# Four up pieces of a feed-forward layer with their products split into halves of the array's rows

## The reference, cut to what matters

```python
h = _causal_depthwise_conv(x @ w_up[l], conv_w[l], conv_b[l])     # w_up: 1024 x 5632, conv over 3 tokens
a, u = jnp.split(h, 2, axis=-1)
ffn = (jax.nn.gelu(a, approximate=False) * u) @ w_down[l]
x = _layer_norm(DEEPNORM_ALPHA * x + ffn, ln_ffn_g[l], ln_ffn_b[l])
```

## Time and profile before

| | |
|---|---|
| median of 3 runs | 1567.59 us (1564.45 to 1567.66) |
| the profiled execution | 1566.09 us, of which the span of the trace is 1564.3 us |
| PE busy | 1515.6 us, 97% of the span |
| DVE, ACT, POOL busy | 1022.0, 691.9 and 435.9 us |
| pieces 4 to 9 of the up projection | 423.63 to 488.91 us from the span's start, six times 10.88 us |

### The profile page before, as it was taken

The page is one execution under the profiler, slowest core; times in us unless marked ns, Lnnn a source line. Parts: engine busy times, 40 slices in busy tenths (PEclk is TensorE's granted clock), DMA queues, the critical chain, the costliest instruction groups (busy, mean ns, idle before and its releaser), DMA issues. The chain is left out here.

```text
span 1564.3 us, 21018 instructions
## 1 busy us (share of the span) xinstructions
PE 1515.6 (97%) x8432; PEld 1300.6 (83%) x8432; DVE 1022.0 (65%) x1547; ACT 691.9 (44%) x1020; POOL 435.9 (28%) x367
## 2 busy tenths in 40 slices
PE   5999998999999999999999999998999999999997
PEld 5778886788888888888988888886788999999886
DVE  7676457769677866678643643338855799985334
ACT  5644346755533354233523344443445544543322
POOL 0024315621511211000260032214342666660002
PEclk9999999999999999999999999999999999999999
DMA  8342112363244523665424332314462123224211
GB/s 310 109 148 92 64 55 95 133 221 118 108 163 161 178 91 121 244 252 204 133 108 148 108 98 91 118 49 161 142 234 87 53 109 109 107 108 162 85 78 54
DMA packets 50987, 203.61 MB, mean 130 GB/s; under 512 B 18528, under 2 KB 18784, under 8 KB 32138
## 3 DMA queue, kind: packets, MB, share of 16 engines
q1 hardware_dynamic: 37346, 172.04, 30.7%
q0 software_dynamic: 8576, 28.29, 5.1%
q10 hardware_dynamic: 4968, 1.94, 0.5%
HBM read 181.24 MB, written 21.00 MB: 129 GB/s over the span
## 5 line engine op out<-in xcount | busy, mean ns | idle before, releaser
L583 PE MATMUL ps<-xl,whi 128*128 128x512 f32 (+1 forms) x1136 | 393.1, 346 | 0.0
L1853 DVE TENSOR_TENSOR wlo<-raw,whi 128x2048 fp32r<-128x2048 f32 x89 | 221.8, 2493 | 142.7 <-ACT whi L1212 142.5
L1212 ACT ACTIVATE whi<-raw 128x512 fp32r<-128x512 f32 (+1 forms) x191 | 232.4, 1223 | 127.6 <-PE ps L584 84.3
L582 PE MATMUL ps<-xh,whi 128*128 128x256 f32 (+1 forms) x768 | 262.4, 342 | 6.2 <-DVE xl L1897 6.2
L584 PE MATMUL ps<-xh,wlo 128*128 128x256 f32 (+1 forms) x768 | 256.8, 334 | 0.0
L583 PEld LDWEIGHTS ps<-xl,whi 128*128 128x128 f32 x1136 | 216.2, 190 | 24.2
L582 PEld LDWEIGHTS ps<-xh,whi 128*128 128x128 f32 x768 | 146.8, 191 | 28.3 <-issue 15.6
L584 PEld LDWEIGHTS ps<-xh,wlo 128*128 128x128 f32 x768 | 146.7, 191 | 14.8
L582 PE MATMUL ps<-xhr,whi 128*128 128x512 f32 (+1 forms) x368 | 136.8, 372 | 0.7 <-DVE xl L1897 0.7
L584 PE MATMUL ps<-xhr,wlo 128*128 128x512 f32 (+1 forms) x368 | 136.4, 371 | 0.0
L2611 DVE TENSOR_TENSOR wlo<-raw,whi 128x512 fp32r<-128x512 f32 x98 | 89.7, 948 | 0.2 <-ACT whi L1212 0.2
(11 more groups left out here) (468 smaller groups left out, 3663.9 us busy)
## 6 DMA issues: line engine op xcount, KB each, us to landing
raw<-in_w_in SPq DMA_DIRECT2D x35, 1024.0 KB, 5.0
raw<-in_ffn_w SPq DMA_DIRECT2D x33, 1024.0 KB, 4.8
raw<-in_ada SPq DMA_DIRECT2D x24, 1024.0 KB, 4.8
raw<-in_w_up SPq DMA_DIRECT2D x22, 1024.0 KB, 4.8
raw<-in_w_down SPq DMA_DIRECT2D x11, 1024.0 KB, 5.3
xd<-X POOLq DMA_DIRECT2D x8, 512.0 KB, 6.9
td<-vr POOLq DMA_DIRECT2D x16, 256.0 KB, 3.6
raw<-td SPq DMA_DIRECT2D x4, 1024.0 KB, 4.8
```

The lines of the kernel that those rows point to most:

```text
L582: pe.e.matmul(o, lh, rh, start=start, stop=False)
L583: pe.e.matmul(o, lh, rl, start=False, stop=False)
L1212: m = ac.e.activation(dst, src, func, **more)
L1853: up(ve.e.tensor_tensor(lo, raw[conv_at[j] % 3][:, :], hi.bitcast(F32), ALU.subtract), "wlo")
```

## The change

Pieces 4 to 7 (j2 = 2 and 3) are made by a new function instead of `pair`. Each of the 48 matmuls of a piece becomes two matmuls of 64 rows. In a first pass the first tile takes rows 0 to 63 of every block and the second tile rows 64 to 127, and their matmuls alternate; in a second pass the two change sides, behind a wait until the first pass is done. Both tiles are complete at the end of the piece, and both banks are taken at its start.

```diff
+            def halved_pair(j, keys, name, values, xh, xl, ch_no):
+
+                h, l = weights(j)
+                bs = [take(keys[m], name, values[m]) for m in range(2)]
+                pe.wait_ge(sig["ch_lo"], ch_no)
+
+                def terms(m, k):
+                    a = k * 256 + P * m
+                    return (h[:, a:a + P], xh[:, k, :]), (h[:, a:a + P], xl[:, k, :]), (l[:, a:a + P], xh[:, k, :])
+
+                for first in range(2):
+                    if first:
+                        pe.wait_ge(sig["pe"], fills.at["halves", j])
+                    for k in range(8):
+                        for i in range(3):
+                            for r in range(2):
+                                m, rows = (first + r) % 2, slice(64 * r, 64 * r + 64)
+                                w, x = terms(m, k)[i]
+                                o = pe.e.matmul(bs[m][:, :], w[rows, :], x[rows, :], start=first + k + i == 0,
+                                                stop=first == 1 and k == 7 and i == 2)
+                                if k == 7 and i == 2 and (first or r):
+                                    done(o, keys[m] if first else ("halves", j))
+                used(j)
+
...
-                    pair(J_UP + 2 * j2 + part, (("up", v), ("up", v + 1)), "cv_2", (v + 1, v + 2), xh2, xl2, 16)
+                    (halved_pair if j2 in (2, 3) else pair)(J_UP + 2 * j2 + part, (("up", v), ("up", v + 1)), "cv_2",
+                                                            (v + 1, v + 2), xh2, xl2, 16)
```

## The result

The changed kernel takes 1569.93 us (median of 18 runs, 1567.41 to 1571.69) against 1566.2 for the kernel before on the same chips. The ratio is 1.0019, with a 95% interval of 1.0012 to 1.0027, so between 1.9 and 4.2 us slower. The profiled execution has a span of 1569.5 us.

A forecast was written before the change was run, and what follows sets the result against it. The prediction took PE, busy 97% of the span, to bound the kernel. Changes of form 0.4, waits 1.2 and a stall of 1.8 made +3.4 us on 1566.4, rounded to 1570, range 1566 to 1576.

The forecast's parts named there:

- A pair costs 0.2267: PE, pieces 4 to 7: two half-row matmuls on opposite halves take 0.2267 us, no change from one full matmul.
- 0.216 of the fp32 pairs: Rival, PE, pieces 4 to 7: a pair costs 0.216 us, as in the attention's fp32 pairs; +1.8 us, 1568.2; 17%.
- 0.240: Rival, PE, pieces 4 to 7: a pair takes two steps of 0.120 us; +5.3 us, 1571.7; 15%.
- serial halves: Rival, PE, pieces 4 to 7: fp32r halves take turns, 0.4533 us a pair, +43.5 us on PE; 8%.
- 0.0133: Part of each full PE matmul's 0.2267 us step beyond streaming 512 columns in 0.2133; assumed to hold up both halves at once.
- Change of form: PE, into half rows before piece 4 and back after piece 7: load not hidden, 0.20 us each, +0.4 us.
- The wait: PE, middle of pieces 4 to 7: waits for its own last matmul before the second pass, 0.30 us each, +1.2 us.
- The chain: ACT and DVE, from piece 6's last matmul start to `wlo` of piece 8: 8.20 us instead of 5.34.
- The stall: PE before piece 10: waits for `wlo`, which DVE's block without slack makes 3.96 us later; 1.8 us.
- Sum: Whole kernel: 0.4 for changes of form, 1.2 for waits and 1.8 for the stall, +3.4 us.
- Behind piece 10: PE after piece 10: later waits follow PE's own results, so nothing absorbs the delay.
- mean of the four executions: Base time the forecast added to: the profiled execution and three runs of the kernel before, 1566.4 us.

The follow-up runs named there:

- odd-pieces kernel: Against the changed kernel, half rows only in pieces 5 and 7, with 4 and 6 as in the kernel before; ratio 1.0011 to the kernel before.
- groups of three: Against the changed kernel, the two halves alternate after every three matmuls and not after each; 1573.40 us in one execution.
- groups of 24: Against the changed kernel, each pass issues all 24 half matmuls of one side before the 24 of the other; 1605.29 us.

## Why the prediction was right, by its steps

- **A pair costs 0.2267.** Measured 0.227, neither the 0.216 of the fp32 pairs nor the 0.240 nor the serial halves, to which the prediction gave 8% and which took 0.45 for two where both lay on the same half. The 0.216, which the prediction also rounds to 0.22, is read from the item of the earlier trace rows: its pairs start at 905.764, 905.980 and 906.196. The 0.2133 and the 0.0133 us follow, as an estimate, from two steps of the kernel before at a granted clock of 1.00: 512 columns cost 0.2267 and 256 cost 0.120, so 256 more cost 0.1067, twice that is 0.2133, and 0.0133 is left. That it nearly goes away in the fp32 pairs was the author's estimate. That whatever holds a matmul up for 0.0133 us holds up both halves at once agrees with the measured 0.227; what it is was not found out.
- **Change of form, 0.20 each.** The starts around it give 0.32 + 0.33 instead of 2 x 0.227, 0.20. The pairs behind it are a few ns slow for about ten steps (2.31 us for the ten from 427.11, where ten of 0.2267 make 2.27), another 0.05. Measured 0.25; 0.5 in sum where 0.4 was forecast. The odd-pieces kernel pays it four times.
- **The wait, 0.30 each.** Measured 0.45 + 0.33 - 0.45 = 0.33, and the same 0.05 behind it: 0.38. 1.5 in sum where 1.2 was forecast. The kernel without the wait and the change of sides shows all of it gone; which of the two holds the 0.38 was not taken apart.
- **The chain.** 8.20 forecast, 8.27 measured, and 1.1 forecast for the end of piece 6 against 1.39. `wlo` of piece 10 was 4.3 us later than before in relation to piece 3, 3.96 forecast. Sorting ACT's work differently shortens the chain, and taking the sums from between breaks it, as the two experiments show.
- **The stall.** 1.8 forecast; 0.5 + 1.5 of TensorE's own, and the rest of 69.24 + 0.05 (the slow steps behind it) - 65.50 is 1.8. That the stall itself came out exact is partly luck: `wlo` of piece 10 was 0.36 us later than forecast (0.07 in the chain, 0.29 in the end of piece 6) and TensorE 0.4 us, and the two cancel. Sum: 3.4 forecast, 3.8 measured in the stretch. The measured ratio stands for 3.0 us, with 3.8 inside its interval.
- **Behind piece 10** TensorE stays later, as forecast, with nothing given back: 621.01 before and 627.84 in this run are the starts of the last up matmul, 6.83 apart, which is the 3.05 from ahead of piece 4 and 3.78. The two profiled executions stay 6.6 to 6.9 apart up to 1080 us and are 5.2 apart at the end. What falls away there is the clock, not the change. In the second block TensorE waits for DVE in both kernels, for 2.16 us between starts from 1078.05 before and for 2.15 from 1084.70 in the changed kernel; behind it the first execution ran at the low clock for a while, and the second didn't:

```profile
1081.00:1085.00 4.00, 3.76 (x10) 2.81 (x10) 2.65 (x2) 1.07 (x1) 0.00 (x0) 0.57 0.52 199
```

```profile
1086.90:1091.00 4.10, 3.87 (x16) 2.89 (x17) 3.35 (x4) 1.81 (x2) 0.00 (x0) 1.00 0.65 233
```

The mean of the four executions then known, 1566.4, proved a better base than the median of three, 1567.59: over 18 runs the kernel before has 1566.2. That the forecast of 1570 lies within 0.1 us of 1569.93 is luck: the medians are 3.7 us apart, the ratio says 3.0, and single executions of one kernel spread over more than 4 us.

## What to carry to other kernels

Splitting a full product over opposite halves of the array's rows gained nothing here: two halves of 512 columns cost what one full matmul cost (0.227 us), every change of form cost 0.25 us more, and every change of sides with its wait 0.38. The order on TensorE that completes two results together instead of one after the other cost as much as that by itself: 2.2 us of the stretch alone, where the half rows alone cost 2.0. To see it, follow the engines that wait for the results, in written order, until one of them has no idle time left, and look for what stands behind its block. Here moving a few sums made that part free, and swapping two instructions left 0.15 us of it.

## What the runs showed of the hardware that was not expected

- TensorE started matmuls of the opposite half ahead of the program's order: by two matmuls in groups of three, which ran side by side at full rate (a pair every 0.227 us), and by three in groups of 24 (430.58), of which only the last four ran beside the other side's.
- After gaps of 2.43 and 2.22 us between starts ahead of piece 10, TensorE went on for seven steps of 0.427 us at a granted clock of 0.50 (494.80 to 497.30 in both), where 0.227 is the step at 1.00, and lost 1.6 us more; after gaps of 1.84 us in the changed kernel and 1.85 in groups of three it did not. The length of the gap does not decide it alone, though: gaps of 2.16 and 2.15 us at the same place of the program were followed by the low clock in one execution and not in the other (the two windows above), and in the profile of before a gap of 1.90 us, from 1112.39, was followed by it too (granted clock 0.58 from 1115 to 1119). So a stall of some 2 us cost nearly twice its length in some of these executions (2.43 less a step of 0.23, and 1.6 more) and not in others.
- In the changed kernel the first ten or so steps after a restart at the full clock are a few ns longer, 0.05 us in all: after the change of form (0.235 us behind 427.11, where 0.227 is usual), the wait (0.235 behind 432.93), the change back (0.235 behind 472.39) and the stall (0.235 behind 495.92).
